# Experts of 64 slots in place of 96, with extra blocks that load their weights again

## The reference, cut to what matters

```python
g_idx = argmax(x @ w_rg + b_rg)                       # group of a token
top_v, top_i = top_k(e_logits of that group, 2)       # two experts in it
top_w = softmax(top_v) * p_group
ys = (silu(xb @ w_gate[e]) * (xb @ w_up[e])) @ w_down[e]   # 1024->512, 1024->512, 512->1024
y  = zeros(T, D).at[row_tok].add(ys * row_w)
x  = x + y
```

## Time and profile before

| | |
|---|---|
| median of 3 runs | 1817.47 us (1816.38 to 1818.67) |
| the profiled execution's own time | 1818.38 us |
| its span | 1816.5 us |
| mean granted clock of TensorE | 0.989 |
| expert stage, first matmul of expert 0 to the end of the span | 1221 to 1816.5 us |

### The profile page before, as it was taken

The page is one execution under the profiler, slowest core; times in us unless marked ns, Lnnn a source line. Parts: engine busy times, 40 slices in busy tenths (PEclk is TensorE's granted clock), DMA queues, the critical chain, the costliest instruction groups (busy, mean ns, idle before and its releaser), DMA issues.

```text
span 1816.5 us, 24241 instructions
## 1 busy us (share of the span) xinstructions
PE 1767.6 (97%) x9846; PEld 1028.9 (57%) x9846; DVE 812.4 (45%) x1694; ACT 386.3 (21%) x835; POOL 130.4 (7%) x128
## 2 busy tenths in 40 slices
PE   8999999999999999999999999969999999999997
PEld 4444545588888888654447884444444444444443
DVE  3486876465435344537735632542222222222234
ACT  4334645200000000225532320021111111111111
POOL 0000000000000000100032221400000000000001
PEclk9999999999999999999999999979999999999998
DMA  5521122321222222121211123817999999999995
GB/s 183 116 62 49 55 83 93 110 82 49 90 93 93 93 93 93 60 93 49 90 48 47 47 61 93 324 73 297 389 393 387 394 384 394 392 399 397 394 410 188
DMA packets 83746, 328.80 MB, mean 181 GB/s; under 512 B 7911, under 2 KB 9060, under 8 KB 75484
## 3 DMA queue, kind: packets, MB, share of 16 engines
q1 hardware_dynamic: 71840, 287.40, 41.9%
q0 software_dynamic: 7632, 26.11, 5.1%
q10 hardware_dynamic: 4204, 14.34, 2.0%
HBM read 305.41 MB, written 22.41 MB: 180 GB/s over the span
## 4 chain that ended last, share of the span: by engine, by line
PE 95%; DVE 2%; DMA 1%; issue 1%; another core or an unknown queue 1%; ACT 0%; SPq 0%; ACTq 0%; DVEq 0%; POOLq 0%
PE ps L1473 13%; PE ps L1050 11%; PE ps L1094 11%; PE ps L918 8%; PE ps L1501 6%; PE ps L1191 6%; PE ps L1481 6%; PE ps L1338 5%; PE ps L1508 3%; PE ps L954 3%; PE ps L914 3%; PE ps L1377 3%; PE ps L1403 3%; PE ps L1202 2%; PE ps L1463 1%; PE ps L973 1%
## 5 line engine op out<-in xcount | busy, mean ns | idle before, releaser
L1473 PE MATMUL ps<-W,yT 128*64 128x512 f32 x1024 | 229.6, 601 | 0.7 <-ACT yT L1956 0.7
L1473 PEld LDWEIGHTS ps<-W,yT 128*64 128x64 f32 x1024 | 71.7, 138 | 143.3 <-issue 142.3
L918 PE MATMUL ps<-hT,W 128*128 128x512 f32 (+1 forms) x336 | 149.3, 595 | 1.7 <-DMA W<-in_w_in 1.7
L1191 PE MATMUL ps<-hT,W 128*128 128x512 f32 x272 | 122.3, 599 | 1.9 <-DVE yT L2505 1.9
L1481 PE MATMUL ps<-W,yT 128*32 128x256 f32 x2048 | 118.1, 381 | 1.6 <-issue 1.6
L1501 PE MATMUL ps<-W,yT 128*64 128x512 f32 x512 | 118.9, 607 | 0.0
L2828 DVE COPY mix<-ps 32x256 f32<-32x256 f32 x124 | 52.3, 421 | 148.4 <-PE ps L1508 147.1
L2809 DVE TENSOR_TENSOR yT<-yT,ps 64x512 f32<-64x512 f32 x32 | 22.1, 691 | 186.9 <-ACT yT L1961 186.9
L918 PEld LDWEIGHTS ps<-hT,W 128*128 128x128 f32 (+1 forms) x336 | 61.2, 188 | 75.2 <-issue 72.9
L1481 PEld LDWEIGHTS ps<-W,yT 128*32 128x32 f32 x2048 | 63.5, 110 | 66.8 <-issue 28.5
L1191 PEld LDWEIGHTS ps<-hT,W 128*128 128x128 f32 x272 | 50.0, 190 | 65.3 <-issue 62.4
(11 more groups left out here) (463 smaller groups left out, 2619.6 us busy)
## 6 DMA issues: line engine op xcount, KB each, us to landing
W<-in_w_expert_gate SPq DMA_DIRECT2D x32, 2048.0 KB, 15.6
W<-in_w_expert_up SPq DMA_DIRECT2D x32, 2048.0 KB, 20.5
W<-in_w_expert_down SPq DMA_DIRECT2D x32, 2048.0 KB
W<-in_w_in SPq DMA_DIRECT2D x16, 2048.0 KB, 7.8
W<-in_w_up SPq DMA_DIRECT2D x8, 2048.0 KB, 7.6
W<-in_w_down SPq DMA_DIRECT2D x8, 2048.0 KB, 7.7
y_scratch<-mix ACTq DMA_DIRECT2D x31, 384.0 KB, 9.2
W<-in_w_out SPq DMA_DIRECT2D x4, 2048.0 KB, 7.8
```

Of the source, the lines that this page charges most:

```text
L918: ins = pe.matmul(ps[0:n, bank, :], wv[:, k, j * P:j * P + n], hT[:, k, :], start=(k == 0), stop=(k == KT - 1))
L1191: ins = pe.matmul(ps[:, bank, :], wv[:, k, j * P:(j + 1) * P], hT[:, k, :], start=(k == 0), stop=(k == KT - 1))
L1473: ins = pe.matmul(ps[64 * part:64 * part + 64, 2, :], xsT[:, x_slot, k, 0:64], wviews[s][part][:, k, :], start=(k == 0), stop=(k == KT - 1))
```

## The change

`BLK` becomes 64. The second part of every expert (slots 64 to 95) goes, with its matmuls, silu, product and copies. Rows from rank 64 on go to extra blocks, which run in the same pipeline right behind expert 31, before any add. An extra block uses buffer set 0; gate and up are loaded in two halves of four k each, as soon as `gu_free` says that the block before has turned its hidden rows, and down when `down_free` says that its result rows are copied.

TensorE's order changes: gate and up of e, turning of the tokens of e + 1, down of e - 1, turning of the hidden rows of e. SyncE's order becomes gate and up of e, then down of e - 1. The rows of down are dealt to partitions as `(p k)` and not `(k p)`, so that a partition reads one run of 16 KB; the hidden rows are written in the matching order.

Token ids are built with an offset, so that empty slots get an id beyond the tensor, which the indirect DMAs leave out. The id also says which choice the row is: `y_scratch` is now 1024 rows, choice times 512 plus token, and POOL scatters the 64 result rows of a block there with an indirect DMA (`spread`). After the last block one pass of eight plain loads on SyncE brings all rows back, and eight adds follow. The matmuls that spread expert 31, `over_scratch` with its zero fill, and the second pass go.

```diff
-BLK = 96
+BLK = 64
-BLOCKS = NE + MAXJOBS
+BLOCKS = NE + MAXJOBS + 1
-        y_dram = nc.dram_tensor("y_scratch", (NE * BLK, D), F32, kind="Internal").ap()
-        over_dram = nc.dram_tensor("over_scratch", (MAXJOBS * BLK, D), F32, kind="Internal").ap()
+        y_dram = nc.dram_tensor("y_scratch", (2 * SEQ, D), F32, kind="Internal").ap()
...
-            source += [io[names[2]].rearrange("l e (k p) n -> (l e) p k n", p=P)]
+            source += [io[names[2]].rearrange("l e (p k) n -> (l e) p k n", p=P)]
...
+            def load_gate_up(e, s):
+                sp.wait_ge(ex["gu"], e - 1)
+                for j in range(2):
+                    sp.dma_start(views[s][j], source[j][e]).then_inc(loads[j][s], 16)
+
+            def load_down(e, s):
+                sp.wait_ge(ex["down"], e - 1)
+                sp.dma_start(views[s][2], source[2][e]).then_inc(wd_load[s], 16)
+
+            load_gate_up(2, 0)
+            with sp.Fori(1, NE // 2 - 1) as it:
+                load_gate_up(it * 2 + 1, 1)
+                load_down(it * 2, 0)
+                load_gate_up(it * 2 + 2, 0)
+                load_down(it * 2 + 1, 1)
+            load_gate_up(NE - 1, 1)
+            load_down(NE - 2, 0)
+            load_down(NE - 1, 1)
...
+                    sp.wait_ge(ov["gu_free"], j + 1)
+                    for half, nm_ in enumerate(("wa", "wb")):
+                        ks = slice(4 * half, 4 * half + 4)
+                        for q in range(2):
+                            sp.dma_start(views[0][q][:, ks, :], source[q][which][:, ks, :]).then_inc(ov[nm_], 16)
+                    sp.wait_ge(ov["down_free"], j + 1)
+                    sp.dma_start(views[0][2], source[2][which]).then_inc(ov["wd"], 16)
+            sp.wait_ge(rows_stored, 1)
+            for c, i in ADDS:
+                sp.dma_start(yg[c][i], y_dram[c * SEQ + i * P:c * SEQ + (i + 1) * P, :]).then_inc(y_gather[c][i], 16)
...
-            pool.wait_ge(y_zero, 16)
...
+            def spread(b, s, nth):
+                pool.wait_ge(ex["ys"], b + 1)
+                pool.tensor_copy(idcol[:, 2 + s:3 + s], row_ids[:, bass.ds(b, 1)]).then_inc(idcol_ready, 1)
+                pool.wait_ge(idcol_ready, nth)
+                pool.sem_inc(fetches, 1)
+                pool.indirect_dma_start(out=y_dram, out_offset=bass.IndirectOffsetOnAxis(ap=idcol[:, 2 + s:3 + s], axis=0),
+                                        in_=ys[0:BLK, s, :], in_offset=None,
+                                        bounds_check=2 * SEQ - 1, oob_is_err=False).then_inc(y_store[s], 16)
...
+            with pool.Fori(0, NE // 2 - 2) as it:
+                for s in range(2):
+                    fetch(it * 2 + (4 + s), s, it * 4 + (3 + 2 * s), it * 2 + (3 + s))
+                    spread(it * 2 + s, s, it * 4 + (4 + 2 * s))
...
             with pool.If(n > 0):
...
+                    fetch(j + (NE + 1), 0, j * 2 + 2 * NE, j + (NE + 1))
+                    spread(j + NE, 0, j * 2 + (2 * NE + 1))
+                    pool.wait_ge(y_store[0], j * 16 + 16 * (NE // 2 + 1))
+            for s in range(2):
+                pool.wait_ge(y_store[s], 16 * (NE // 2))
+            pool.sem_inc(rows_stored, 1)
...
             with pe.Fori(1, NE // 2 - 1) as it:
                 for s in range(2):
-                    expert(it * 2 + s, s, it)
+                    expert(it * 2 + s, s, it * 16 + 16, it * 16 + (16 + 16 * s))
+                    expert_ahead(it * 2 + s, s, it * 16 + 16 * s)
+                    turn_rows(it * 2 + s)
...
                 with pe.Fori(0, n) as j:
...
+                    pe.wait_ge(ov["wa"], j * 32 + 32)
+                    gate_up(0, range(4))
+                    pe.wait_ge(ov["wb"], j * 32 + 32)
+                    gate_up(0, range(4, KT))
+                    pe.wait_ge(ex["hid"], j + (NE + 1))
+                    turn_hidden()
+                    pe.sem_inc(ov["gu_free"], 1)
+                    pe.wait_ge(ex["hT"], j + (NE + 1))
                     pe.wait_ge(ov["wd"], j * 16 + 16)
+                    pe.wait_ge(ex["ys"], j + NE)
+                    down(0)
+                    pe.wait_ge(ex["ys"], j + (NE + 1))
+                    pe.sem_inc(ov["down_free"], 1)
```

More of the change, by code:

```diff
@@ L379, in build @@
         idcol_ready = sem("idcol_ready")
-        EXPERT = ("xt", "xT", "gua", "gub", "silua", "silub", "hida", "hidb", "hta", "htb", "hTa", "hTb",
-                  "downa", "downb", "ysa", "ysb")
+        EXPERT = ("xt", "xT", "gu", "silu", "hid", "ht", "hT", "down", "ys")
         ex = {n: sem(f"ex_{n}") for n in EXPERT}
-        ov = {n: sem(f"over_{n}") for n in ("wgu", "wd", "id", "gather", "store", "free")}
+        ov = {n: sem(f"over_{n}") for n in ("wa", "wb", "wd", "gu_free", "down_free")}
         y_gather = [[sem(f"y_gather{c}_{i}") for i in range(NT)] for c in range(2)]
@@ new lines, in expert, with expert_ahead @@
+            def expert(e, s, loads_of, loads_ahead):
+                pe.wait_ge(ex["xT"], e + 1)
+                pe.wait_ge(wg_load[s], loads_of)
+                pe.wait_ge(wu_load[s], loads_of)
+                gate_up(s)
+                pe.wait_ge(gather[1 - s], loads_ahead)
+                turn_tokens(1 - s)
+            def expert_ahead(e, s, loads_ahead, second=False):
+                pe.wait_ge(ex["hT"], e)
+                pe.wait_ge(wd_load[1 - s], loads_ahead)
+                if not second:
+                    pe.wait_ge(ex["ys"], e - 1)
+                down(1 - s)
@@ L1539, in _, with turn_rows @@
+            def turn_rows(e):
+                pe.wait_ge(ex["hid"], e + 1)
+                turn_hidden()
             pe.wait_ge(gather[0], 16)
-            turn_tokens(xs[0:BLK, 0, :], ex["xt"])
+            turn_tokens(0)
             pe.wait_ge(route_act, 7)
-            for e in range(2):
-                expert(e, e, 0, first=(e == 0))
+            expert(0, 0, 16, 16)
+            turn_rows(0)
+            expert(1, 1, 16, 32)
+            expert_ahead(1, 1, 16, second=True)
+            turn_rows(1)
@@ L1965, in rows_a, with rows @@
-            def rows_a(n, s):
-                act.wait_ge(ex["downa"], n)
+                act.wait_ge(ex["gu"], n)
+                act.activation(sgate, ps[0:64, 2, :], ACT.Silu).then_inc(ex["silu"], 1)
+            def rows(n, s):
+                act.wait_ge(ex["down"], n)
                 act.activation(ys[0:64, s, 0:512], ps[0:64, 4, :], ACT.Copy)
-                act.activation(ys[0:64, s, 512:1024], ps[64:128, 4, :], ACT.Copy).then_inc(ex["ysa"], 1)
-            def expert(e, s, turns_of, first=False, last=False):
+                act.activation(ys[0:64, s, 512:1024], ps[64:128, 4, :], ACT.Copy).then_inc(ex["ys"], 1)
@@ L1983, in expert @@
[L1983 to L1988 removed]
+                if e:
+                    rows(e, 1 - e % 2)
             with act.Fori(1, NE // 2 - 1) as it:
                 for s in range(2):
[L1991 to L1992 removed]
@@ L1993, in _ @@
-            act.wait_ge(turn_done, turned_by(T_N2, NT - 1) + 1)
-            act.activation(last_hotT, ps[0:BLK, 7, :], ACT.Copy).then_inc(turn_evac, 1)
-            expert(NE - 1, 1, NE // 2 - 1, last=True)
+                    hidden_silu(it * 2 + (2 + s))
+                    act.wait_ge(y_store[s], it * 16)
+                    rows(it * 2 + (1 + s), s)
+            hidden_silu(NE)
+            for e in range(NE - 2, NE):
+                act.wait_ge(y_store[e % 2], 8 * NE - 16)
+                rows(e + 1, e % 2)
@@ L2874, in _ @@
-            then(dve.tensor_tensor(r_far, r_far, r_last, ALU.add))
-            dve.tensor_copy(opos[:, :, :], r_far).then_inc(turn_src, 1)
-            for s in range(2):
-                expert(NE - 2 + s, s, NE // 2 - 1, last=(s == 1))
-            def add_last(i):
-                dve.wait_ge(last_rows, i + 1)
-                dve.wait_ge(add_done, LAST_ADDS.index((1, i)) + 1)
-                at = x[:, i, :].rearrange("p (a b) -> p a b", a=2)
-                dve.tensor_tensor(at, at, ps[:, 2 * i:2 * i + 2, :], ALU.add).then_inc(add_done, 1)
```

361 lines of the change are left out of this document (99 added, 262 removed).

## The result

The kernel after takes 1806.28 us (median of 4 runs, 1802.27 to 1808.57) against 1816.93 for the kernel before on the same chip (1815.58 to 1818.67): ratio 0.9938, 95% interval 0.9918 to 0.9959. The forecast said 1829, slower by 0.6%; the change made the kernel faster by 0.6%. Timed again on two other occasions, each beside the kernel before on the same chip, it gave 1807.80 (ratio 0.9942, 0.9928 to 0.9955) and 1806.59 (0.9941, 0.9925 to 0.9958). The profiled execution took 1808.57 us for a span of 1806.5, against a forecast span of 1828.5.

A forecast was written before the change was run, and what follows sets the result against it. The prediction took TensorE and the DMA as near-equal limits before, the DMA after: start 1232.7, 30 experts at 16.95 to X = 1741.2, tail 87.3, span 1828.5, plus 1 gives 1829 us; range 1800 to 1852, own range 1822 to 1836.

The forecast's parts named there:

- the fullest engine: Expert loop: every load waits for the engine with most rows; four filled slots, gather 1.50, scatter 0.75, period 16.95 us.
- the first rival: Expert loop: only filled rows cost, spread evenly over engines; period 16.0 to 16.4, time 1801 to 1813 us; chance 0.28.
- the even spread: Expert loop: filled rows evenly over engines, 2.25 each; gather 0.84 us, scatter 0.42 to 0.84; chance 0.28.
- as dear as the gather: Expert loop rival: the scatter costs 1.50 us like the gather; period 17.7, time 1852 us; chance 0.20.
- The price of the old store: Kernel before: a 96-row store costs 1.1 us of DMA time, 0.19 us a row on its engine; used for the scatter.
- Weights at 14.70 us: Expert loop: one expert's 6.29 MB of weights in 16 KB runs at 428 GB/s take 14.70 us of DMA time.
- TensorE's limit and the DMA's: Kernel before, per expert: TensorE sets 17.84 us, DMA traffic costs 18.1 us, a third of a microsecond apart.
- the half clock: Loop: TensorE slow after waits, 15.3 us an expert, hidden by DMA; rival where it lasts, 1861 us, chance 0.04.
- nothing interrupts the stream: Weight loads of 30 experts: bytes flow from 1232.7 without a break, the last down landing at X = 1741.2 us.
- The tail: From the last down's landing (X) to the end: three extra blocks, scatter, final pass, last add and store, 87.3 us.
- a load of 12.7 us: Extra blocks 1 and 2: serial gate and up load, 2.9 + 9.8, within 19.5 us a block (bounds 17.5 and 22).
- X + 19.6: Tail: block 0 has turned its hidden rows and frees its slot 19.6 us after the last down lands at X.

The follow-up runs named there:

- full gather: Kernel after, but empty slots fetch token 511, so every gather moves 64 rows; the scatter still leaves empty slots out: 1834.45 us, ratio to before 1.0145.
- 4 KB runs: Kernel after with down weights read in 4 KB rows dealt as (k p) and hidden rows written plainly: 1807.76 us, ratio to before 1.0002.
- warm loop: Kernel after plus four unused matmuls per expert, filling TensorE's wait for weights: 1811.28 us, ratio to before 1.0010.

## Why the prediction was wrong

**The failed step** is the one on the fullest engine: "four neighbouring slots per engine, so that the first engines carry four filled rows for nearly every expert (or empty slots cost as much as filled ones) ... I take 16.95". Measured is 16.12, in the 16.0 to 16.4 of the first rival, whose forecast of 1801 to 1813 us holds the result. Over 30 experts this makes 24.9 us; start, hole and tail together make 2.9 the other way. The full gather shows it: were the first engines full already, or did empty slots cost as much as filled ones, 34 more rows would have cost nothing, and they cost 0.80 us. What the runs put in its place is a cost by the number of rows that move: 0.023 us a gathered one, 0.004 a written one, and 0.7 us an expert without a price. The forecast took the fullest engine over the even spread on an argument about rank order that no row bore out.

The Trainium skill, page "DMA: Bandwidth & Descriptors", section "Why a DMA increments its semaphore by 16 and not by 1", says that the software queue can give each engine ceil(partitions/16) of the partitions. It says so of some direct copies, and the gathers here are indirect, which the forecast passed over. How the slots lie on the engines was not read here, but the time that the forecast drew from that rule did not come: the cost goes with the number of filled rows.

**The sizes inside it.** The even spread's price of the gather, 0.84 us for 32 rows, is borne out by the full gather's 0.80 for 34. The scatter, 0.42 to 0.84 there, costs 0.16 for 37 added rows; the rival "as dear as the gather", 0.20 of the chance, is excluded for added rows, and its 17.7 us as the period. The price of the old store did not carry over. Weights at 14.70 us are near the fit's 14.6. So the rival's 16.0 to 16.4 holds the measured period with one term of it too high and 0.7 us that it does not have; that these cancel is luck.

**Right:** TensorE's limit and the DMA's lie close together in the kernel before (17.84 against 17.5 to 17.8, measured with TensorE relieved, or 18.0 by its own rate); three blocks; TensorE waits in the loop and the DMA is full; the half clock is there in the loop and costs nothing. The rule of the Trainium skill's page "TensorE: Matmul & The Clock Gate", section "HAM oscillation — how this bites in real kernels", cold at every wait for weights, agrees with the trace for the waits of 3.85 us and more; the experts between them waited up to 1.56 us and ran at full clock, hence the granted clock of 0.90. In this loop it cost nothing.

**The stream's start and end.** Start: the load of expert 2 was issued at 1227.28, where 1231.3 was forecast; expert 0's gate and up took 8.64 us, not 9.94, and began at 1218.61 in place of 1221.26, since the first gather was issued 1.7 us sooner (1212.72) and came faster. End: the forecast said that nothing interrupts the stream. The order on SyncE does: expert 31's down waits for that of expert 29, which ended at 1705.0, and all of block 0's loads stand behind it. Block 0's gate and up also need expert 30's hidden rows turned, which ended at 1705.6, so the order is not their only hold. In the loop the same wait is hidden, because the gate and up of a later expert are ahead of it in the queue.

**The tail, near as a sum, by the wrong chain and with luck.** 90.6 us against 87.3. TensorE's timeline of block 1 and the last down of block 2:

```profile
1733.23 5.35 PE L1488 MATMUL ps<-W,yT 128*64 128x512 f32 x16 [0.69 <-DVE yT L2775]
1740.54 1.51 PE L1466 MATMUL ps<-ident,mix 96*128 96x96 f32 x8 [1.96 <-ACT mix L1940]
1742.97 9.28 PE L1474 MATMUL ps<-W,yT 128*64 128x512 f32 x32 [0.93 <-DVE yT L2763]
1754.01 0.62 PE L1481 MATMUL ps<-ident,yT 64*128 64x64 f32 x5 [1.76 <-DVE yT L2770]
...
1775.84 6.48 PE L1488 MATMUL ps<-W,yT 128*64 128x512 f32 x16 [0.69 <-DVE yT L2775]
```

The forecast took a load of 12.7 us as what sets a block. TensorE does not wait for it here: the weights, released at 1732.14, are there when gate and up start at 1742.97. A block is TensorE's own chain, down of the block before (5.35 at half clock), 1.96 for the copies of its result, tokens 1.51, their copies 0.93, gate and up 9.28, silu and product 1.76 (the product 0.35 dearer than the earlier trace rows said, for its permuted write), turn 0.62, and hand-overs. That makes 22.1 us from block 1's release to block 2's and 20.9 to where block 2 turns its hidden rows, 43.0 instead of 39. Block 0 is 3.4 sooner than its X + 19.6 (1732.14), the last down with its copies 2.3 dearer; the scatter took 4.5 instead of 5.6, the final pass 13.5 instead of 13.0, the last add and store 5.5 instead of 4.5. These errors of both signs add up to 3.3 us. Where the forecast's 19.5 us a block does come near, 19.3 for the second step in another trace of this kernel, it is by TensorE's full clock and not by the load.

## What to carry to other kernels

When two limits lie within a few per cent, cut the work of both or expect the difference of the two, and price the moved bytes per kind: beside a full load stream, 4 KB rows that an indirect DMA gathers cost 0.023 us each here, rows that it writes 0.004, and rows that it leaves out are not moved. What the two DMAs of an expert cost without rows was not measured. Where issues take long and short steps by turns, take a period over an even number of them and check it one issue earlier: otherwise it can be off by 0.3 us in 16. Serial blocks at the end cost more than the same work in the pipeline (19.4 against 16.1 us here), by the waits and the clock of one chain; releasing buffers sooner helped only once the fetch on the other queue came sooner too. Filling a hole in the DMA did not pay here, since that load overtook one that was needed first.

## What was not expected of the hardware

- Writes by the indirect DMA raised the total from 411 to 413 and from 408 to 414 GB/s in the windows of 1400 to 1600 us, where gathered rows lowered it to 394.
- The old traffic moved at 394 GB/s beside a busy TensorE and at 402 with TensorE's work cut, in the window of 1300 to 1400 us. The cause is open.
- Slots that the indirect DMAs leave out remain as packets: q0 counts 7600 whether they move rows or not.
- The kernel before ran in 1809 us on some chips and in 1817 on others; variants close to the kernel after took 1807.76 (4 KB runs) and 1811.28 (warm loop) on the former, and the run with a fourth block less 19.4 us for that block gives an estimate of 1806. So most of the gain of 0.6% may be absent there. Why the kernel before differs was not found, and the kernel after was not timed there.
